# A ninth slot for raw weights, denser gate steps, and a new order in the wide places of an expert pipeline

## The chip, the cores and the metric

One core of a Trainium2 chip (trn2). The time is that of the whole program on the device in microseconds, once per run; the profiled execution is one run of its own. TensorE (PE) multiplies, VectorE (DVE) and ScalarE (ACT) work on tiles in SBUF and PSUM, GpSimd (POOL) here issues the indirect transfers, SyncE (SP) issues the plain ones, and sixteen DMA engines move the bytes.

## What is computed

One layer of a streaming encoder over 512 tokens of width 1024: a norm, one wide projection, two kinds of attention, an output projection with residual, and then a mixture of 32 experts, of which every token uses 4. All but the last part takes the first quarter of the time. The expert part, cut to what matters:

```python
logits = (hf @ w_router + b_router).astype(jnp.float32)
top_vals, top_idx = lax.top_k(logits, TOP_EXPERTS)       # 4 of 32
gates = jax.nn.softmax(top_vals, axis=-1)
...
def expert_block(args):
    tok, g, e = args
    xb = h_pad[tok]                                      # the tokens of expert e
    gu = xb @ w_gu[e] + b_gu[e]                          # 1024 -> 2048
    glu = jnp.minimum(gu[:, :D_EXPERT], SWIGLU_LIMIT)
    lin = jnp.clip(gu[:, D_EXPERT:], -SWIGLU_LIMIT, SWIGLU_LIMIT)
    act = glu * jax.nn.sigmoid(SWIGLU_ALPHA * glu) * (lin + 1.0)
    return (act @ w_down[e] + b_down[e]) * g[:, None].astype(h.dtype)
```

## The kernel before, in words

**Chunks.** The weights of an expert are 12 MB in float32, read in 12 chunks of 1 MB (128 partitions x 2048): eight of the gate and up weights (c = 0 to 7, `NG`) and four of the down weights (c = 8 to 11). `chunk_no` numbers all 384 in the order in which they are used: the gate and up chunks of expert i, then the down chunks of expert i - 1, then those of i + 1, and so on. Number 0 to 7 are the first expert's, 8 to 15 the second's.

**The path of a chunk.** SP loads it into one of `RAW` = 8 raw slots (`load_chunk`, line 825); the slot is chunk number modulo `RAW`, and SP waits until VectorE is done with the chunk that had the slot before. ScalarE rounds it to a high half (`split_hi`, line 833) into one of `HL` = 4 buffers `whl`; it waits for the landing, and for TensorE's use of the chunk four before. VectorE subtracts, which gives the low half (`split_lo`, line 838), and frees the raw slot. TensorE multiplies both halves (`chunk_products`, line 2125). Precision of float32 is had this way from products of rounded halves. All transfers of weights are in SP's one queue.

**Wide and narrow.** The 32 experts are put in an order (`place_experts`) in which 17 places are wide (up to 128 rows; three products per pair of halves, 12 matmuls of 512 columns to a chunk) and 15 are narrow (`NARROW`: 3, 4, 7, 8, 11, 12 ... 27, 28, 30; up to 64 rows, whose high and low rows share the array, 8 matmuls to a chunk, and two folds add the halves up). The first three experts are fixed; the others depend on the counts.

**Order within place i.** Each engine has its own queue, written out by hand. PE: bias and eight gate and up chunks of expert i (`gate_up`), among them the transposes of the activations of i - 1 (`turn_a`) and the search for the rows of i + 2 (`find_both`); transposes of the gathered rows of i + 1 (`turn_x`); bias and four down chunks of i - 1 (`down`). ACT (`act_round`): the eight high halves, then those of the down chunks 8 to 10; the gate (`gated`, line 1314), the high halves of the transposed rows (`turn_x_hi`, 1296), the selector (`pick_gu`), and then the high half of the twelfth chunk, c = 11. DVE (`dve_round`): eight low halves, three more, the clamp of the linear part (`lin`, line 1798), the low halves of the transposed rows (`turn_x_lo`, 1779), the product of gate and linear part (`activate`, 1806), and then the twelfth low half. In narrow places the twelfth halves stand ahead of `gated` and `lin` already. GpSimd gathers the rows of i + 2 (line 1019) and adds the results of i - 2 to the output (line 1028), both indirect, in its own queue.

**The start of the expert part.** After the last token block is routed, VectorE makes the ranks, finds the rows of experts 0 and 1, then spreads the gates over the experts (`spread_gates`): softmax over the 4 chosen, a comparison of 512 columns, a product of 512, a sum to 128, and then copies that `turn_g` transposes. Only after that does it come to the first low half. Chunks 0 to 5 are loaded ahead, 6 and 7 after the last normalised rows have been written to DRAM; chunk 8 waits for the first low half. GpSimd clears the first gather buffer `xg0` as soon as attention is over, and prepares small tables (`tie`, `ordered`, `spread`, `left`) behind that. PE runs filler matmuls (`keep_warm`) between the short steps.

**Memory.** Addresses are laid out by hand. `xg0` lies at `o_qb + 54272`, the scratch of the gates (`one`, `onek`) and the scratch of the row search `ohd` just above it, the transposed gate table `gT` at `o_qb + 12288`, where the raw biases `bg_raw` were.

## Time and profile before

| what | us |
|---|---|
| median of 3 runs (1439.07 to 1441.06) | 1440.77 |
| the profiled execution | 1441.15 |
| its span | 1439.0 |
| PE busy in the span | 1348.1 (94%) |
| DVE busy | 1254.8 (87%) |
| ACT busy | 1118.7 (78%) |
| POOL busy | 207.4 (14%) |
| VectorE's low halves of the weights, 384 of 2286 ns | 862.9 |
| ScalarE's high halves, 384 of 1916 ns | 725.8 |
| read from DRAM | 440.89 MB |

The page cuts the span into 40 slices of 36 us and gives the busy share of each engine as a digit; 9 is 90% or more. The expert part begins in the tenth slice, near 340 us. In the answers quoted below `idle before <-X` is the time that an engine stood idle ahead of an instruction and what ended it. Busy times of PE are modelled from pipelined matmuls. A wait is put down to the last of several releasers.

### The profile page before, as it was taken

How to read it: one execution, taken by the hardware profiler on the slowest of the kernel's cores; microseconds unless marked ns; L12 is line 12 of the kernel's file. 1: busy time of each engine (PE TensorE's matmuls, PEld its weight loads, DVE VectorE, ACT ScalarE, POOL GpSimd, SP SyncE). 2: the span in 40 equal slices, each digit the busy share in tenths (PEclk: the TensorE clock that was granted, in tenths of full speed). 3: DMA queues.
4: the chain of work that ended last, by engine and by line, in shares of the span. 5: the costliest groups of instructions: out<-in, count | busy, mean ns of one | idle time of the engine just before them, and what ended most of it. 6: DMA issues, size and time to landing. Idle time of an engine off the chain costs nothing. (4 is left out here: it accounts for less than half of the span.)

```text
span 1439.0 us, 18474 instructions
## 1 busy us (share of the span) xinstructions
PE 1348.1 (94%) x6573; PEld 1089.5 (76%) x6576; DVE 1254.8 (87%) x1314; ACT 1118.7 (78%) x1225; POOL 207.4 (14%) x134
## 2 busy tenths in 40 slices
PE   6999878999999999999998999999899989998996
PEld 5887766776787878778876887787778768876785
DVE  4799779548989999999899998999999999899995
ACT  5666564455788988988898888888888988898884
POOL 1112000011011211111210111111111111210131
PEclk9999979999999999999999999999999999999999
DMA  5422111148899999999999999999999999999992
GB/s 153 146 74 59 33 71 45 44 159 310 337 348 363 409 411 387 394 403 391 390 395 396 392 375 401 394 389 379 403 383 390 382 389 388 393 387 386 398 396 66
DMA packets 85349, 446.41 MB, mean 310 GB/s; under 512 B 18432, under 2 KB 23552, under 8 KB 36032
## 3 DMA queue, kind: packets, MB, share of 16 engines
q1 hardware_dynamic: 73424, 428.32, 75.1%
q0 software_dynamic: 9216, 16.81, 4.6%
q8 instruction: 54, 0.88, 0.2%
q10 hardware_dynamic: 2608, 0.01, 0.1%
q14 instruction: 47, 0.39, 0.1%
HBM read 440.89 MB, written 20.97 MB: 321 GB/s over the span
## 5 line engine op out<-in xcount | busy, mean ns | idle before, releaser
L838 DVE TENSOR_TENSOR whl<-wraw,whl 128x2048 fp32r<-128x2048 f32 x384 | 862.9, 2286 | 73.1 <-ACT whl L833 71.7
L833 ACT ACTIVATE whl<-wraw 128x2048 fp32r<-128x2048 f32 x384 | 725.8, 1916 | 136.8 <-PE ps L2125 88.2
L2125 PE MATMUL ps<-whl,xT 128*128 128x512 f32 x2640 | 634.0, 394 | 13.6 <-DVE whl L838 11.6
L2125 PEld LDWEIGHTS ps<-whl,xT 128*128 128x128 f32 x2640 | 488.5, 188 | 129.3 <-DVE whl L838 19.4
L2125 PE MATMUL ps<-whl,aT 128*128 128x512 f32 x1248 | 297.9, 394 | 5.2 <-DVE whl L838 5.2
L2125 PEld LDWEIGHTS ps<-whl,aT 128*128 128x128 f32 x1248 | 235.5, 190 | 60.4 <-DVE whl L838 10.1
L1028 POOL DMA_INDIRECT out_dram<-ysb,idx x32 | 84.5, 2641 | 667.2 <-ACT ysb L1325 667.2
L1019 POOL DMA_INDIRECT xg<-h_rows,idx x32 | 80.0, 2501 | 262.5 <-DVE idx L1767 258.5
L1879 PE MATMUL ps<-W,HT 128*128 128x512 f32 (+1 forms) x184 | 73.9, 402 | 5.4 <-DVE W L610 4.4
L1881 PE MATMUL ps<-W,HT 128*128 128x512 f32 (+1 forms) x184 | 70.3, 382 | 0.0
L1880 PE MATMUL ps<-W,HT 128*128 128x512 f32 (+1 forms) x184 | 70.3, 382 | 0.0
L1507 DVE TENSOR_REDUCE nmax<-ps 128x1 f32<-128x128 f32 (+3 forms) x64 | 31.2, 487 | 30.8 <-PE ps L1953 30.0
L1314 ACT ACTIVATE acts<-ps 128x1024 f32<-128x1024 f32 x32 | 32.9, 1030 | 16.7 <-PE ps L2125 15.2
L1879 PEld LDWEIGHTS ps<-W,HT 128*128 128x128 f32 x184 | 36.5, 198 | 11.1 <-issue 5.2
L2082 PE MATMUL ps<-ident,xg 128*128 128x128 f32 x256 | 34.0, 276 | 9.0 <-DVE gslot L1773 7.7
L2082 PEld LDWEIGHTS ps<-ident,xg 128*128 128x128 f32 x256 | 28.6, 140 | 17.9 <-DVE gslot L1773 13.7
L1169 ACT ACTIVATE raw<-ps,nmax 128x384 f32<-128x384 f32 (+2 forms) x40 | 24.1, 604 | 22.5 <-DVE nmax L1507 22.3
L1325 ACT ACTIVATE ysb<-ps,gslot 128x1024 f32<-128x1024 f32 x32 | 35.1, 1098 | 8.3 <-DMA out_dram<-ysb,idx 7.3
L1881 PEld LDWEIGHTS ps<-W,HT 128*128 128x128 f32 x184 | 36.4, 198 | 6.7
L1179 ACT ACTIVATE sq<-ps 128x384 f32<-128x384 f32 (+2 forms) x28 | 14.7, 524 | 34.5 <-PE ps L1891 34.2
L1806 DVE SCALAR_TENSOR_TENSOR acts<-acts 128x1024 f32<-128x1024 f32 x32 | 39.1, 1221 | 1.5
L1880 PEld LDWEIGHTS ps<-W,HT 128*128 128x128 f32 x184 | 36.7, 199 | 4.6
(294 smaller groups left out, 1428.3 us busy)
## 6 DMA issues: line engine op xcount, KB each, us to landing
wraw<-in_w_gu_dram SPq DMA_DIRECT2D x256, 1024.0 KB, 15.5
wraw<-in_w_down_dram SPq DMA_DIRECT2D x128, 1024.0 KB, 13.5
WR<-in_w_in_dram SPq DMA_DIRECT2D x20, 512.0 KB, 3.8
WR<-in_w_o_dram SPq DMA_DIRECT2D x8, 512.0 KB, 4.0
xs<-in_x_dram SPq DMA_DIRECT2D x4, 512.0 KB, 8.1
WR<-in_x_dram SPq DMA_DIRECT2D x4, 512.0 KB, 3.6
out_dram<-WR SPq DMA_DIRECT2D x4, 512.0 KB, 2.6
h_rows<-WR SPq DMA_DIRECT2D x4, 512.0 KB, 2.6
```

Source lines behind the costliest of these rows:

```text
L833: act.activation(whl[:, n % HL, 0, :], wraw[n % RAW], ACT.Copy).then_inc(chunk_hi, 1)
L838: eng.tensor_tensor(whl[:, n % HL, 1, :], wraw[n % RAW], whl[:, n % HL, 0, :].bitcast(F32), ALU.subtract).then_inc(chunk_lo, 1)
L1019: pool.indirect_dma_start(xg[j % 2], None, hd, bass.IndirectOffsetOnAxis(ap=idx[:, j:j + 1], axis=0), bounds_check=SEQ - 1, oob_is_err=Fal ...
L1028: pool.indirect_dma_start(out[0], bass.IndirectOffsetOnAxis(ap=idx[:, e:e + 1], axis=0), ysb, None, bounds_check=SEQ - 1, oob_is_err=False ...
L1314: act.activation(acts[:, 0, :].rearrange("p (a n) -> p a n", a=2), ps[:, GU:GU + 2, :], ACT.Gelu_apprx_sigmoid).then_inc(sig_ok, 1)
L1325: act.activation(ysb.rearrange("p (a n) -> p a n", a=2), ps[:, dn_bank(e):dn_bank(e) + 2, :], ACT.Copy, scale=gslot[:, e:e + 1]).then_inc( ...
L1806: dve.scalar_tensor_tensor(out=acts[:, 2, :], in0=acts[:, 0, :], scalar=GLU_TOP, in1=acts[:, 1, :], op0=ALU.min, op1=ALU.mult).then_inc(ac ...
L1879: pe.matmul(dst, a[0], b[0], start=k_first, stop=False)
L1880: pe.matmul(dst, a[0], b[1], start=False, stop=False)
L1881: return pe.matmul(dst, a[1], b[0], start=False, stop=k_last)
L2082: ins = pe.transpose(ps[:, TP + b, k * P:(k + 1) * P], xg[j % 2][:, (4 * b + k) * P:(4 * b + k + 1) * P], ident)
L2125: ins = pe.matmul(bank, a[x_][j], w[:, b, j, 512 * q:512 * q + 512], start=False, stop=last and j == nj - 1 and n == len(parts) - 1)
```

## The change

- `RAW` goes from 8 to 9. The ninth slot takes the place of `xg0` and the gates' scratch; SP waits for the chunk nine before, and the stream's first load without a wait is chunk 8. The count of landings to wait for is worked out per slot.
- `xg0` moves onto the raw biases, so GpSimd waits for the three steps of the biases (`bg_ok`, 3) before it clears it. `gT` moves into the last third of `acts`, `ohd` to a place of its own; `one`, `onek` and `gate` go.
- The gates: the difference to the largest logit, the exponential, a product with the 0/1 mask of chosen experts, sum, reciprocal and product are done over all 128 columns (4 blocks x 32 experts) instead of over the 16 chosen and then spread.
- In wide places the high half of the twelfth chunk comes before `gated` on ScalarE, and its low half right behind `lin`, ahead of the transposed rows and `activate`, on VectorE.

```diff
-RAW, HL = 8, 4
+RAW, HL = 9, 4
...
-        wraw = [place(f"wraw{s}", [P, 2048], F32, offset=base + 8192 * s if s < 6 else o_qb + 66560 + 8192 * (s - 6))
-                for s in range(RAW)]
+        wraw_at = [base + 8192 * s for s in range(6)] + [o_qb + 66560, o_qb + 74752, o_qb + 54272]
+        wraw = [place(f"wraw{s}", [P, 2048], F32, offset=wraw_at[s]) for s in range(RAW)]
...
-        xg0 = place("xg0", [P, D], F32, offset=o_qb + 54272)
+        xg0 = place("xg0", [P, D], F32, offset=o_qb + 12288)
...
-        gT = place("gT", [3 * E, 2, T * P], F32R, offset=o_qb + 12288)
+        gT = place("gT", [3 * E, 2, T * P], F32R, offset=o_qb + 40960)
...
         def load_chunk(eng, r, e, c, at_=None):
             n = chunk_no(e, c)
             w = wraw[n % RAW]
-            after(eng, chunk_lo, PER_ROUND * r + n - RAW + 1)
+            after(eng, chunk_lo, PER_ROUND * r + max(n - RAW + 1, 0))
...
-            act.wait_ge(landed[n % RAW], 16 * (PER_ROUND // RAW * r + n // RAW + 1))
+            per_slot = len(range(n % RAW, PER_ROUND, RAW))
+            act.wait_ge(landed[n % RAW], 16 * (per_slot * r + n // RAW + 1))
...
-                    if not is0(r) or chunk_no(e, c) >= RAW:
+                    if not is0(r) or chunk_no(e, c) >= NG:
                         load_chunk(sp, r, e, c, ids_at.get(e))
...
             pool.wait_ge(values_ok, values_no("A", T - 1, HA - 1))
+            pool.wait_ge(bg_ok, 3)
             pool.memset(xg[0], 0.0).then_inc(xg_clear, 1)
...
-            act.activation(gate, gate, ACT.Exp).then_inc(gates_exp, 1)
+            act.activation(gden, gden, ACT.Exp).then_inc(gates_exp, 1)
...
                     if narrow(i):
                         gu_low_half(r, i)
                     else:
+                        split_hi(act, r, i - 1, NCH - 1)
                         gated(r, i)
                     if i + 1 < E:
                         turn_x_hi(r, i + 1)
                         pick_gu(r, i + 1)
-                    split_hi(act, r, i - 1, NCH - 1)
                     if narrow(i):
+                        split_hi(act, r, i - 1, NCH - 1)
                         gated(r, i)
...
-            dve.tensor_tensor(gate, top8[:, :, 0:TOPE], top8[:, :, 0:1].to_broadcast([P, T, TOPE]),
-                              ALU.subtract).then_inc(gates_in, 1)
+            dve.tensor_tensor(gden, lg, top8[:, :, 0:1].to_broadcast([P, T, E]), ALU.subtract).then_inc(gates_in, 1)
...
                 dve.wait_ge(gates_exp, 1)
-                link(dve.tensor_reduce(gsum, gate, AX.X, ALU.add))
+                link(dve.tensor_tensor(gden, gden, selm, ALU.mult))
+                link(dve.tensor_reduce(gsum, gden, AX.X, ALU.add))
                 link(dve.reciprocal(gsum, gsum))
-                link(dve.tensor_tensor(gate, gate, gsum.unsqueeze(2).to_broadcast([P, T, TOPE]), ALU.mult))
-                link(dve.tensor_tensor(one.rearrange("p t k e -> p (t k) e"),
-                                       over_experts(0, E), over_choices(idxf, E), ALU.is_equal))
-                link(dve.tensor_tensor(onek.rearrange("p t k e -> p (t k) e"),
-                                       one.rearrange("p t k e -> p (t k) e"), over_choices(gate, E), ALU.mult))
-                link(dve.tensor_reduce(gden, onek.rearrange("p t k e -> p t e k"), AX.X, ALU.add))
+                link(dve.tensor_tensor(gden, gden, gsum.unsqueeze(2).to_broadcast([P, T, E]), ALU.mult))
...
                     if not narrow(i):
                         lin(r, i)
+                        split_lo(dve, r, i - 1, NCH - 1)
                     if i + 1 < E:
                         turn_x_lo(r, i + 1)
                     if narrow(i):
                         split_lo(dve, r, i - 1, NCH - 1)
                         lin(r, i)
                     activate(r, i)
-                    if not narrow(i):
-                        split_lo(dve, r, i - 1, NCH - 1)
```

## Rows read from the trace of the kernel before

**Rows 1.** The page, slices of 36 us: busy tenths of the DMA engines

```profile
DMA  5422111148899999999999999999999999999992
```

**Rows 2.** Stretches: length, PE, PEld, DVE, ACT, POOL busy, clock, DMA share, GB/s

```profile
500.00:600.00 100.00, 97.50 (x456) 78.69 (x455) 93.92 (x61) 86.67 (x76) 14.44 (x6) 1.00 1.00 396
700.00:800.00 100.00, 94.26 (x437) 74.84 (x436) 92.31 (x60) 86.65 (x75) 13.09 (x6) 1.00 0.99 393
```

**Rows 3.** Groups, 500 to 1400 us: instruction, count | busy, mean ns | idle before

```profile
L838 DVE TENSOR_TENSOR whl<-wraw,whl 128x2048 fp32r<-128x2048 f32 x322 | 723.1, 2286 | 63.3 <-ACT whl L833 62.2
L833 ACT ACTIVATE whl<-wraw 128x2048 fp32r<-128x2048 f32 x322 | 608.6, 1917 | 114.6 <-PE ps L2125 67.6 <-DMA wraw<-in_w_down_dram 42.5 <-DMA wraw<-in_w_gu_dram 4.0
```

**Rows 4.** Weight loads, issue to landing, issued 345-412, 412-460, 600-1400 us

```profile
DMA to landing us min/median/max: 4.8/5.2/6.6
...
DMA to landing us min/median/max: 6.5/7.8/9.1
...
DMA to landing us min/median/max: 12.2/15.6/18.6
```

**Rows 5.** Stretches of 4 us behind expert 10, columns as in rows 2

```profile
704.00:708.00 4.00, 4.00 (x20) 3.30 (x19) 4.00 (x3) 3.05 (x2) 0.00 (x0) 1.00 0.85 349
732.00:736.00 4.00, 4.00 (x19) 3.27 (x18) 2.76 (x3) 4.00 (x5) 0.69 (x1) 1.00 1.00 424
```

**Rows 6.** Timeline, start of the experts: start, length, engine, line [idle before]

```profile
340.71 0.69 DVE L1684 TENSOR_TENSOR onek<-one,gate 128x512 f32<-128x512 f32 x1
341.43 1.04 DVE L1686 TENSOR_REDUCE gden<-onek 128x128 f32<-128x512 f32 x1
344.23 1.07 PE L2082 MATMUL ps<-ident,xg 128*128 128x128 f32 x8 [0.80 <-DMA xg<-h_rows,idx]
346.01 1.27 PE L2153 MATMUL ps<-bgs,sel 128*128 128x512 f32 x4
```

**Rows 7.** Gathers into xg, issue to landing: the first; those of 500-1400 us

```profile
DMA to landing us min/median/max: 4.0/4.0/4.0
...
DMA to landing us min/median/max: 9.9/10.2/10.6
```

**Rows 8.** Timeline, transposes of the rows of expert 1

```profile
371.67 1.06 PE L2082 MATMUL ps<-ident,xg 128*128 128x128 f32 x8 [0.45 <-issue]
```

**Rows 9.** Timeline, VectorE at expert 1: the clamp, and the twelfth half

```profile
401.38 1.22 DVE L1798 TENSOR_SCALAR acts<-ps 128x1024 f32<-128x1024 f32 x1
404.84 6.69 DVE L838 TENSOR_TENSOR whl<-wraw,whl 128x2048 fp32r<-128x2048 f32 x3
```

**Rows 10.** Three weight loads: ns of issuing, first and last start; issue to landing

```profile
L825 SPq DMA_DIRECT2D wraw<-in_w_gu_dram x1: 328/328/328, 407.2 to 407.2; - x1
...
L825 SPq DMA_DIRECT2D wraw<-in_w_down_dram x1: 327/327/327, 409.4 to 409.4; - x1
...
DMA to landing us min/median/max: 5.1/5.1/5.1
...
L825 SPq DMA_DIRECT2D wraw<-in_w_down_dram x1: 328/328/328, 411.6 to 411.6; - x1
...
DMA to landing us min/median/max: 5.9/5.9/5.9
```

**Rows 11.** Timeline at expert 13: splits after the product, PE's twelfth chunk, next bias

```profile
806.05 11.09 DVE L838 TENSOR_TENSOR whl<-wraw,whl 128x2048 fp32r<-128x2048 f32 x5
808.39 2.11 PE L2125 MATMUL ps<-whl,aT 128*128 128x512 f32 x8 [0.55 <-DVE whl L838]
810.33 1.07 PE L2153 MATMUL ps<-bgs,sel 128*128 128x512 f32 x4
```

**Rows 12.** Timeline at the last expert, and the last rows

```profile
1409.38 1.23 DVE L1806 SCALAR_TENSOR_TENSOR acts<-acts 128x1024 f32<-128x1024 f32 x1
...
1412.73 1.28 DVE L1790 TENSOR_TENSOR xT<-ps,xT 128x512 fp32r<-128x512 f32 x2
...
1428.27 1.11 ACT L1325 ACTIVATE ysb<-ps,gslot 128x1024 f32<-128x1024 f32 x1 [7.29 <-DMA out_dram<-ysb,idx]
```

More of the change, by code:

```diff
@@ L391, in build @@
         at["free"] = kept
-        one = place("one", [P, T, TOPE, E], F32, offset=o_qb + 58368)
-        onek = place("onek", [P, T, TOPE, E], F32, offset=o_qb + 60416)
         gden = place("gden", [P, T, E], F32, offset=o_qb + 62464)
@@ L400, in build @@
         gfcol = place("gfcol", [P, KD], F32)
+        ohd = place("ohd", [P, T, P], BF16, offset=at["free"])
         gh = place("gh", [P, 5, HD], F32)
@@ L439, in build @@
         idxf = place("idxf", [P, T, TOPE], F32)
-        gate = place("gate", [P, T, TOPE], F32)
         gsum = place("gsum", [P, T], F32)
@@ L452, in build @@
         passed = place("passed", [P, 2 * E], U32)
-        ohd = place("ohd", [P, T, P], BF16, offset=o_qb + 58368)
         cmax = place("cmax", [P, 1], F32)
@@ L1668, in read_counts @@
                 dve.tensor_copy(crow, ps[:, TP + 1, T * E:(T + 1) * E]).then_inc(counts_read, 1)
-            def over_experts(e0, n):
-                return iota[:, e0:e0 + n].unsqueeze(1).to_broadcast([P, T * TOPE, n])
-            def over_choices(tile, n):
-                return tile.rearrange("p t k -> p (t k)").unsqueeze(2).to_broadcast([P, T * TOPE, n])
             def spread_gates():
                 dve.wait_ge(gates_exp, 1)
-                link(dve.tensor_reduce(gsum, gate, AX.X, ALU.add))
+                link(dve.tensor_tensor(gden, gden, selm, ALU.mult))
+                link(dve.tensor_reduce(gsum, gden, AX.X, ALU.add))
                 link(dve.reciprocal(gsum, gsum))
-                link(dve.tensor_tensor(gate, gate, gsum.unsqueeze(2).to_broadcast([P, T, TOPE]), ALU.mult))
-                link(dve.tensor_tensor(one.rearrange("p t k e -> p (t k) e"),
-                                       over_experts(0, E), over_choices(idxf, E), ALU.is_equal))
-                link(dve.tensor_tensor(onek.rearrange("p t k e -> p (t k) e"),
-                                       one.rearrange("p t k e -> p (t k) e"), over_choices(gate, E), ALU.mult))
-                link(dve.tensor_reduce(gden, onek.rearrange("p t k e -> p t e k"), AX.X, ALU.add))
+                link(dve.tensor_tensor(gden, gden, gsum.unsqueeze(2).to_broadcast([P, T, E]), ALU.mult))
                 dve.tensor_copy(gdup[:, :, 0:2, :], gden.unsqueeze(2).to_broadcast([P, T, 2, E])).then_inc(gdup_ok, 1)
```

## The prediction

> **What bounds the kernel now.** I read the page's slices first [rows 1]: from the ninth slice on, which is the expert stage, the DMA digit stays at 9 until the last slice. The stretches of 100 us [rows 2] say it more sharply: the DMA engines are busy 0.99 to 1.00 of the time, TensorE 94 to 98 us of 100, VectorE 92 to 94 (one early and one later stretch stand there). Nothing has room, so which is the bound must be read from who is late. The groups of instructions [rows 3] show that ScalarE, whose high halves start each chunk's work, waits 42.5 + 4.0 us for landings and 67.6 us for TensorE (its four split buffers); VectorE waits only for ScalarE. So in some places a weight chunk is late and in others TensorE is.
>
> The decisive view is the time from the issue of a weight load to its landing [rows 4]. Each load is 1 MB and is issued when VectorE has finished with the chunk eight before it. Where the DMA engines had run dry, a load lands in 4.8 us (345 to 412 us). From 600 us on it takes 12.2 us at least and 15.6 in the median. A megabyte takes 2.47 us at the best rate that the stretches of 4 us show (1.049 MB / 424 GB/s, [rows 5]), so even the quickest load finds about (12.2 - 4.8) / 2.47 = 3 others ahead of it, and the median 4 to 5. After about 412 us the engine that delivers the last part of each load therefore never stands idle. That it is one lagging part and not all 16 follows from the other row of [rows 5]: at 704 to 708 us the mean busy share is 0.85 while loads still wait 12 us. Some engines had emptied every issued load; the last one had not. A load counts as landed only with its last part, so the rate of the slowest engine sets the rate of the stage.
>
> The Trainium skill (DMA: Bandwidth & Descriptors, Latency and other measured facts) says that two of the sixteen DMA engines are usually slower in traces, with the reason uncertain. The views here have no time for a single engine, so the trace bears out the inequality but not which engine.
>
> **Part 1, the ninth slot.** It lets each load be issued one VectorE split earlier. While the last engine is always busy that changes the order of nothing: a longer queue in front of the same server. It pays only once, in the stage's first 70 us, where loads land in 4.8 to 6.6 us and TensorE is the bound. The last time that the engines run dry in the kernel before is around 407 to 412 us. The load issued at 411.6 us lands after 5.9 us, at 417.5 [rows 10]. With nine slots it may be issued when the load before it was, at 409.4, the end of the first split of expert 2. If it finds the engines dry it lands 5.1 us later [rows 10], at 414.5: 3.0 us earlier. If the load ahead of it is still under way (issued at 407.2 at the earliest without a new order, [rows 10]; 5.1 us later it is 412.3, then 2.47 to 3.1 for the next), it lands at 415.0: 2.5 earlier. From there on no load waits for a slot, and every later landing, the last one too, keeps that lead. The order of part 3 decides between the two: at expert 1, a wide place, VectorE makes the twelfth lower half at 404.84 now, behind the clamp (401.38, 1.22 us), the transposed rows and the product [rows 9]. Moved ahead of rows and product it ends at about 404.8 instead of 407.1, so the load ahead is issued 2.3 us earlier. I take **-2.9 us**, with -2.5 as the bound without that help.
>
> **Part 2, the start.** The gates lose four DVE steps over 128 x 512 and over 16 columns and gain three over 128 x 128. Of the removed ones the comparison and the product, of one shape, took 0.69 us each and the sum 1.04 [rows 6]; the new ones are near the 0.2 to 0.3 us of steps of that size. VectorE reaches its first split about 2.1 us sooner. The cover of this saving is TensorE: its first transposes wait for the gathered rows until 344.23 (0.80 us idle, <-DMA), and then it is in steady work through the bias products (346.01, 1.27 us) up to the first expert product at 347.3 [rows 6]. So the saving ends in a wait for the rows, and is worth nothing at 347. The VectorE queue then runs about half a microsecond ahead, which removes the 0.45 us wait of TensorE at 371.67 [rows 8] (for the permuted tables, that VectorE reads behind two splits): worth 0.2 to 0.4 us.
>
> Against it stands chunk 8. Before, it waited for VectorE's first split; now it goes out right behind chunks 6 and 7, ahead of the first gather. In the kernel before the gather landed in 4.0 us; among full queues later it takes 9.9 to 10.6 [rows 7]. No run shows it with one load beside it. The load holds each engine for 2.47 us and nothing more is issued before VectorE's first split ends at about 344, so the gather can be 0 to 2.5 us late. I take 1.5, nearer the upper end, since [rows 7] shows that gathers do wait behind weight loads. Every step after it up to 412 us is a TensorE chain, so this delays the consumer, and with it the slots and all later landings: 1.5 less the 0.2 above, **+1.3 us**, bounds -0.4 and +2.3.
>
> The Trainium skill (DMA: Bandwidth & Descriptors, Queues, rings and completion order) says that a DMA engine takes turns between its queues packet by packet, a packet being a bundle of rows. By that rule the gather would wait for one whole packet of the load at most, which is the 2.5 us end; by single rows it would be nearer 1 us.
>
> The moved memory costs nothing that I find: the clearing of the first gather buffer now waits for the bias splits, and these end on VectorE some five microseconds before GpSimd gets there; the gate table in the last third of the activations is read before the first product of activations is written.
>
> **Part 3, the order in wide places.** It moves no work away, only one high half (1.92 us of ScalarE) and one low half (2.29 us of VectorE, [rows 3]) ahead of gate, rows and product, 17 times. What is queued behind: the gate, the transposed rows and the selector on ScalarE, rows and product on VectorE. Who waits for those is TensorE, with the next expert's bias (needs the product) and first chunk (needs the rows). Where the expert before is narrow TensorE gets there soonest: at expert 13 the bias of the next runs at 810.33, while the product is ready at about 806.1 now (the five splits that follow it start at 806.05) and at 808.4 then, by the 2.29 us of a split [rows 3, 11]. There the move takes away a wait of 0.55 us for the twelfth lower half at 808.39 [rows 11], 7 such places, 4 us of TensorE's time. With the DMA as the bound this is given back as waiting for landings in the narrow places: 0. If the DMA had room it would count in full. Landings allow the move: in the wide places ScalarE stands behind TensorE and not behind the twelfth chunk's landing (its long landing waits all stand in narrow ones).
>
> At the last place it costs. Expert 31 has no transposed rows to put in the gap. Now: product 1409.38 to 1410.6, twelfth lower half to 1412.8 (2.29 us, [rows 3]), which covers transposes and high half of the activations, their lower halves from 1412.73 (1.28 us), and then the next split [rows 12]. After: half from 1409.3 to 1411.5, product to 1412.75, and then the transposes (start to high half 0.8 us, high half 0.6) stand uncovered; the lower halves start at about 1414.2 instead of 1412.73. The chain goes on through the first down chunk of 31, the fold, the rows of 30, and their scatter, for which the last rows wait 7.29 us [rows 12]; all of it moves by **+1.5 us** (bounds 0 and +2.2, the whole move of the product).
>
> **Sum.** -2.9 + 1.3 + 1.5 = -0.1 us on the profiled execution of 1441.15 us (span 1439.0, 2.15 around it). The median of the three runs is 0.38 lower, so 1440.77 - 0.1 = 1440.7 us. The unknown terms at their ends give -2.9 - 0.4 + 0 = -3.3 and -2.5 + 2.3 + 2.2 = +2.0, so 1437.5 to 1442.8.
>
> **Rivals.**
> A, the mean of the engines binds and not the last one: then slot and order fill the dips, such as the 15% of 704 to 708 us [rows 5]. The stretches of 100 us leave 0 to 2% idle, 1% in the mean [rows 2], over 900 us some 9 us, and the start and end terms still cost 2.8 less the 2.9: 1440.7 - 9 = 1431.7. For it: the dips do fall behind wide places, where VectorE frees no slot for five microseconds. Against: the 12.2 us minimum [rows 4]. Chance 0.14.
> B, the terms at start and end come out at their lower bounds (the gather isn't disturbed, the gap at the end is covered): 1437.5, faster by 0.23%. Chance 0.09.
> C, slower: the first gather is caught as the later ones are. It then takes 10.2 us and not 4.0 [rows 7], TensorE's first expert product comes 6.2 us late, and 6.0 - 2.9 + 1.5 = +4.6: 1445.4. It decides at a gather over 4.5 us late. Against it: only one extra load is there to wait for. Chance 0.08.
> D, the ninth slot isn't used as said (a load still waits for an older split, or the lead is lost before 412 us): -2.9 drops out, 1443.6, at the edge of slower. Chance 0.05.
>
> **How the numbers follow.** The forecast, 1440.7 within 1437.5 and 1442.8, has 0.64; A 0.14, B 0.09, C 0.08, D 0.05. A measurement of this kernel tells about 0.2% (2.9 us) from no change. Faster: A, B, half of what the forecast has below 1438: 0.26. Slower: C, half of D and a little above the forecast's end: 0.12. Same: 0.62. The range leaves out A's better part and C: 1433.0 to 1443.5.
>
> **What would show it.** Right: landings of 4.8 us gone after 405 us and the time from issue to landing up by about 2.5 us in the rest of the stage (median near 18), DMA share and GB/s unchanged; ScalarE's waits for landings about as long as now; the 0.55 us waits before the twelfth chunk gone; the first gather over 4.0 us; a gap on VectorE behind the last product. Wrong: ScalarE's 46 us of landing waits shrink by a third or more while GB/s rises (A); or the first expert product at 353 (C).

## The result, and the profile after

| | before | changed |
|---|---|---|
| median of 18 runs each, us | 1439.22 (1436.94 to 1441.21) | 1441.59 (1437.54 to 1446.27) |
| ratio of the changed kernel to the one before | | 1.0018 [1.0010, 1.0025] |
| the profiled execution | 1441.15 | 1437.54 |
| its span | 1439.0 | 1435.3 |

The change makes the kernel slower by 2.4 us (1.4 to 3.6 by the interval). The forecast was no difference, 1440.7 us, within 1433.0 and 1443.5. The two profiled executions say the opposite of the medians: that of the changed kernel was the quickest of its 18, 4 us below its median, and that of before lies 1.9 us above its own. Spans of the two traces must not be subtracted. What can be compared is stages, and for that more traces of both were taken (below). Two later executions, one of e9 with 2216.8 us and one of the kernel before with 1863.6 us, ran at a mean granted clock of 0.56 and 0.67 and are left out of the ratios.

The page of the changed kernel: span, busy times, the DMA engines' busy tenths, and weight loads with the median time from issue to landing.

```profile
span 1435.3 us, 18473 instructions
PE 1346.7 (94%) x6573; PEld 1088.1 (76%) x6576; DVE 1254.2 (87%) x1312; ACT 1118.1 (78%) x1225; POOL 211.0 (15%) x134
...
DMA  5422111148899999999999999999999999999991
...
wraw<-in_w_gu_dram SPq DMA_DIRECT2D x256, 1024.0 KB, 18.6
wraw<-in_w_down_dram SPq DMA_DIRECT2D x128, 1024.0 KB, 16.4
```

The same stretches of 100 us as in [rows 2], with the same columns:

```profile
500.00:600.00 100.00, 97.94 (x458) 79.05 (x457) 94.39 (x61) 86.65 (x76) 14.46 (x6) 1.00 1.00 396
700.00:800.00 100.00, 95.47 (x436) 75.99 (x436) 91.85 (x59) 86.20 (x75) 14.00 (x6) 0.98 1.00 393
```

The transfers move the same 396 and 393 GB/s as in [rows 2]. Weight loads from issue to landing, issued at 345 to 412, 412 to 460 and 600 to 1400 us, as in [rows 4]:

```profile
DMA to landing us min/median/max: 4.6/6.1/7.2
...
DMA to landing us min/median/max: 4.9/7.1/7.6
...
DMA to landing us min/median/max: 13.7/18.6/21.0
```

In the steady part a load is under way for 3.0 us more in the median, 18.6 against 15.6. That is about one load's time: 2.47 us at the best rate [rows 5], and 2.65 us at the 396 GB/s of the stage (1.049 MB / 396 GB/s, an estimate). The ninth slot is used, and what it holds is a place in a queue. The groups of 500 to 1400 us, as in [rows 3]: ScalarE's high halves, and TensorE's products.

```profile
L831 ACT ACTIVATE whl<-wraw 128x2048 fp32r<-128x2048 f32 x324 | 613.4, 1916 | 121.7 <-PE ps L2113 75.0 <-DMA wraw<-in_w_down_dram 41.6 <-DMA wraw<-in_w_gu_dram 5.0
...
L2113 PE MATMUL ps<-whl,aT 128*128 128x512 f32 x1059 | 251.0, 393 | 1.5 <-DVE whl L836 1.4
```

ScalarE waits 41.6 + 5.0 us for landings, where it was 42.5 + 4.0. TensorE's wait for low halves is 1.4 us in that stretch; in the kernel before the same group stood idle for 5.2 us, so nearly all of the 4 us of waits for the twelfth lower half [rows 11] are gone. ScalarE's waits for TensorE grew from 67.6 to 75.0 us in the same stretch; what the order is worth in time is taken up below.

The start. The first gather from issue to landing (4.0 us in [rows 7]), and TensorE's first transposes with the idle time ahead of them (0.80 us in [rows 6]):

```profile
DMA to landing us min/median/max: 6.4/6.4/6.4
...
343.44 1.06 PE L2070 MATMUL ps<-ident,xg 128*128 128x128 f32 x8 [2.87 <-DMA xg<-h_rows,idx]
```

The end, the timeline at the last expert, which answers to [rows 12]: start, length, engine, line, idle time ahead.

```profile
1399.78 3.79 PE L2113 MATMUL ps<-whl,aT 128*128 128x512 f32 x16
...
1402.44 2.28 DVE L836 TENSOR_TENSOR whl<-wraw,whl 128x2048 fp32r<-128x2048 f32 x1
1404.64 1.22 DVE L1795 SCALAR_TENSOR_TENSOR acts<-acts 128x1024 f32<-128x1024 f32 x1
1405.91 1.16 PE L2079 MATMUL ps<-ident,acts 128*128 128x128 f32 x8 [2.34 <-DVE acts L1795]
1406.82 5.51 PE L2113 MATMUL ps<-whl,aT 128*128 128x512 f32 x16
1407.35 1.29 DVE L1779 TENSOR_TENSOR xT<-ps,xT 128x512 fp32r<-128x512 f32 x2 [1.50 <-ACT xT L1305]
...
1424.22 1.11 ACT L1324 ACTIVATE ysb<-ps,gslot 128x1024 f32<-128x1024 f32 x1 [7.07 <-PE ps L2113]
```

The low half now runs ahead of the product (L1795), the product is 2.28 us later, and nothing covers that: TensorE stands idle for 2.34 us ahead of the transposes of the activations, and VectorE for 1.50 us behind the product. Then comes something that the forecast did not have. Sixteen matmuls took 3.79 us at 1399.78, and 5.51 us at 1406.82. The stretches of the same part (columns as in [rows 2]) show why:

```profile
1399.00:1406.00 7.00, 4.66 (x22) 3.54 (x21) 6.76 (x4) 4.69 (x4) 0.00 (x0) 1.00 0.18 75
1406.00:1411.00 5.00, 5.00 (x19) 4.14 (x20) 3.65 (x4) 3.43 (x4) 0.00 (x0) 0.66 0.03 15
1411.00:1416.00 5.00, 5.00 (x23) 4.11 (x22) 5.00 (x3) 4.20 (x3) 0.00 (x0) 1.00 0.00 0
```

The granted clock is 1.00 up to the wait and 0.66 in the 5 us behind it, so most of that stretch was at 1.2 GHz instead of 2.4. TensorE had stood idle for 2.34 us before. The transposes right behind the wait still took 1.16 us, as in the kernels with the old last place; the low clock came after them. The Trainium skill (TensorE: Matmul & The Clock Gate, HAM oscillation — how this bites in real kernels) describes a kernel whose TensorE waits some 3 to 5 us for data in every round and comes back at the lower clock. This trace is like it in kind, with 0.66 behind a shorter wait; in e10 (below) the clock is 1.00 behind a wait of 2.36 us, so it is seen here in some traces and not in all.

### The profile page after: what moved, and what is told of

It is laid out like the page before. It is cut to its first block and busy times, and to the rows that moved or that the text cites. A ratio compares the mean times of both kernels' runs of the same rounds, so it can differ in the third digit from the quotient of the medians.

```text
span 1435.3 us, 18473 instructions
## 1 busy us (share of the span) xinstructions
PE 1346.7 (94%) x6573; PEld 1088.1 (76%) x6576; DVE 1254.2 (87%) x1312; ACT 1118.1 (78%) x1225; POOL 211.0 (15%) x134
## 5 line engine op out<-in xcount | busy, mean ns | idle before, releaser
L1018 POOL DMA_INDIRECT xg<-h_rows,idx x32 | 84.6, 2643 | 262.1 <-DVE idx L1756 258.1
L1795 DVE SCALAR_TENSOR_TENSOR acts<-acts 128x1024 f32<-128x1024 f32 x32 | 39.0, 1220 | 1.5
L970 POOL TENSOR_TENSOR rstd<-ss,half 128x8 f32<-128x8 f32 (+1 forms) x16 | 23.3, 1458 | 107.1 <-DVE ss L1429 107.1
## 6 DMA issues: line engine op xcount, KB each, us to landing
wraw<-in_w_gu_dram SPq DMA_DIRECT2D x256, 1024.0 KB, 18.6
```

The costliest lines, as they stand in the source:

```text
L1018: pool.indirect_dma_start(xg[j % 2], None, hd, bass.IndirectOffsetOnAxis(ap=idx[:, j:j + 1], axis=0), bounds_check=SEQ - 1, oob_is_err=Fal ...
L1795: dve.scalar_tensor_tensor(out=acts[:, 2, :], in0=acts[:, 0, :], scalar=GLU_TOP, in1=acts[:, 1, :], op0=ALU.min, op1=ALU.mult).then_inc(ac ...
```

## Stages of all traces

Two marks cut the expert stage: the first high half of the stage (chunk 0) and that of chunk 376, the first down chunk of expert 30, eight chunks from the last. In the changed kernel they are

```profile
328.93 3.70 ACT L831 ACTIVATE whl<-wraw 128x2048 fp32r<-128x2048 f32 x2
...
1392.23 1.92 ACT L831 ACTIVATE whl<-wraw 128x2048 fp32r<-128x2048 f32 x1 [1.61 <-DMA wraw<-in_w_down_dram]
```

so 1063.30 us lie between them, and 43.1 us from the second to the end of the span. A third mark, chunk 16, is the first down chunk; it stands behind the gate and up chunks of the first two experts. The same for every trace, in us; the experiments are told below.

| trace | slots | last place | chunk 0 to 16 | chunk 0 to 376 | chunk 376 to end | chunk 0 to end |
|---|---|---|---|---|---|---|
| before | 8 | old | 59.75 | 1067.19 | 40.0 | 1107.2 |
| before, second trace | 8 | old | 58.40 | 1064.69 | 40.6 | 1105.3 |
| changed | 9 | new | 60.03 | 1063.30 | 43.1 | 1106.4 |
| changed, second trace | 9 | new | 60.00 | 1063.06 | 43.0 | 1106.1 |
| e2, last place as before | 9 | old | 59.94 | 1063.17 | 40.9 | 1104.1 |
| e3, all places as before | 9 | old | 59.80 | 1063.89 | 40.9 | 1104.8 |
| e4, before with the new order | 8 | new | 58.45 | 1063.86 | 43.0 | 1106.9 |
| e6, as e2 | 8 | old | 58.12 | 1063.97 | 40.9 | 1104.9 |
| e7, as e2 | 7 | old | 57.90 | 1066.39 | 40.5 | 1106.9 |
| e9, as e2, gather first | 9 | old | 59.41 | 1063.32 | 40.8 | 1104.1 |
| e10, before, new last place | 8 | new | 58.45 | 1066.73 | 42.2 | 1108.9 |
| e11, changed, filler at the end | 9 | new | 63.20 | 1066.76 | 42.1 | 1108.9 |

Chunk 0 itself comes at 328.9 to 333.7 us, whatever the kernel; the part ahead of it makes most of the difference between executions. Three of the traces are disturbed between the first marks: in that of before, from which the forecast was made, and in that of e9 TensorE's granted clock was 0.79 in the mean of 374 to 382 us (some 1.4 us lost, by 59.75 against 58.40), and e11 had a low clock twice (below). The other rows agree to 0.3 us in the first column for either number of slots, and to 0.9 in the last but one for either last place. In between executions differ by up to 2 us: e10, whose change lies behind chunk 376, needs 1066.73 us up to there, and the second trace of before 1064.69. The clock goes with that. From 632 to 640 us the granted clock is 0.79 in e10 and in the first trace of before, which need 1008.3 and 1007.4 us from chunk 16 to 376; it is 1.00 in the other three traces with eight slots (the second of before, e4, e6), which need 1005.4 to 1006.3. No run shows that this is the whole of the difference.

The same marks show when the loads become the bound. ScalarE's first wait for a landing comes at 593 us in e6 and at 623 us in the changed kernel. Up to chunk 80, at 568 us, the changed kernel stays 1.9 us behind e6, counted from chunk 0; at chunk 150, at 758 us, it is 0.9 us ahead. So the delay of the start is seen at once and in full, and the lead of the slot only where landings are waited for.

## Experiments

Ratios are to the kernel before, run on the same chip beside them; medians are of 11 or 12 runs unless said. The kernel before had medians of 1439.58 (e1 to e4), 1439.96 (e5 to e8) and 1440.08 (e9 to e12). An interval is about 0.001 to either side, so the difference of two ratios is good to some 0.0014, 2 us.

**e1, the changed kernel again**, without an edit.

> The changed kernel once more, for its distance to the kernel before and for a second profile of it. Its first profiled execution (1437.5 us) was its quickest of 18, four below their median, so what makes the usual execution slower has not been seen yet. Theory 1 (loss at the end of the program): ratio 1.001 to 1.0025 again, and in the trace the lead of 3 to 4 us of the expert stage is there until the last expert and is lost there. Theory 2 (the ninth load in the queues slows the transfers in some executions): the second trace shows the stage between 600 and 1400 us longer than in the kernel before by 2 to 5 us. Either way the landing time of the loads has a median of 18 to 19 us.

Measured: 1441.80 us, 1.0020 [1.0007, 1.0033]. The loss is of the kernel. The second theory is out: the stage up to chunk 376 is as short as in the first trace (1063.06 us). The first holds for the end (43.0 us), but the lead up to there is 1.6 us against e5 (below) and not 3 to 4.

**e2, the last place as before.** The changed kernel, with the old order at i = E - 1 alone.

```diff
                     else:
-                        split_hi(act, r, i - 1, NCH - 1)
+                        if i < E - 1:
+                            split_hi(act, r, i - 1, NCH - 1)
                         gated(r, i)
+                        if i == E - 1:
+                            split_hi(act, r, i - 1, NCH - 1)
...
                         lin(r, i)
-                        split_lo(dve, r, i - 1, NCH - 1)
+                        if i < E - 1:
+                            split_lo(dve, r, i - 1, NCH - 1)
...
                     activate(r, i)
+                    if i == E - 1:
+                        split_lo(dve, r, i - 1, NCH - 1)
```

> The changed kernel with the old order in the last place alone (expert 31: gate and product ahead of the twelfth halves), the new order in the other 16 wide places. Theory 1: the trace of the changed kernel lost 3.1 us there (1.5 for the uncovered transposes, 1.6 for matmuls at half clock behind TensorE's wait of 2.3 us), so this comes out 3.1 us below the changed kernel, about 0.7 below the kernel before (ratio 0.9995). Theory 2: only 1.5 to 3 below the changed kernel's, and the scatter from run to run stays.

Measured: 1438.87 us, 0.9999 [0.9990, 1.0008]; 2.9 us below e1. Its timeline at the end, the transposes of the last activations and the products behind them:

```profile
1405.65 1.16 PE L2085 MATMUL ps<-ident,acts 128*128 128x128 f32 x8 [0.18 <-DVE acts L1798]
1406.57 3.92 PE L2119 MATMUL ps<-whl,aT 128*128 128x512 f32 x16
```

The wait of 2.34 us is 0.18 and the matmuls take 3.92 us, not 5.51. By the table the end is 40.9 instead of 43.0 us. With one place of the seventeen undone the whole net loss is gone.

**e3, the old order in all wide places**, nine slots and the new gates kept: the two moves of the change undone for every i.

> The changed kernel with the old order in all wide places: nine slots, moved memory and the new gate steps alone. Theory 1: the lead of the slot without the end's loss, 2.5 less 0.3 at the start: 2.2 us below the kernel before (ratio 0.9985). Theory 2: the slot is what costs, so it is 1 to 3 us above the kernel before (ratio 1.001 to 1.002) and scatters by 8 us as the changed kernel does.

Measured: 1440.04 us, 1.0002 [0.9991, 1.0013]. The gain that I expected of slots and gates alone isn't there. Against e2 it is 1.2 us slower by the medians and 0.7 by the traces (1104.8 against 1104.1): small, and inside the intervals.

**e4, the new order alone.** The kernel before with the moves of the change in all wide places, eight slots, old gates.

> The kernel before, with eight slots and its old gate steps, and only the new order in the wide places. Theory 1: no lead (at most 0.2 us from the earlier slot at expert 1) and the whole loss at the end: 3 us above the kernel before (ratio 1.002). Theory 2: only the 1.5 us of the end, ratio 1.001, with the small scatter of the kernel before.

Measured: 1440.48 us, 1.0011 [1.0000, 1.0023]. The end takes 43.0 us as in the changed kernel. Up to chunk 376 it needs 1063.86 us, 0.8 less than the undisturbed trace of before. Its ratio is that of e10 below, which moves the last place alone (1.0011 and 1.0012), so by the medians the other sixteen places are worth nothing.

**e5, the kernel before, a second trace.** One run.

> The kernel before, once more, for a second trace of it: four kernels with parts of the change, one with eight slots among them, were all about 3.3 to 4 us ahead of its first trace at the last expert, which a slot can't explain. Theory: the first trace of the kernel before was an unlucky one (half clock for 3.4 us at 374 us and again at 634 us), and this one gets to the high half of chunk 376 some 1065.5 us after that of chunk 0 (the first took 1067.2), so that the real lead of the changed kernel is 2 to 2.5 us. Rival: 1067 again, the lead is 4 us and is lost elsewhere.

Measured: 1437.50 us; 1064.69 us from chunk 0 to 376, where I had expected 1065.5. Against this trace the changed kernel reaches chunk 376 1.4 to 1.6 us sooner, and not 3.9.

**e6, eight slots, and e7, seven**, in the kernel of e2.

```diff
-RAW, HL = 9, 4
+RAW, HL = 8, 4
```

> The changed kernel with the old order at the last expert (the one that took 1438.9) and eight slots instead of nine, all else equal (moved memory, new gate steps, new order in 16 wide places). Theory 1 (a longer queue before the same last DMA engine, lead won once): 2.5 us more, 1441.4. Rival (the slot's lead is lost or was never bound): no more than 0.5 us.

> The same with seven slots. Theory 1: another 2.5 us, 1444, and the quickest landing after 600 us takes about 10 us. Rival (the slots hold a reserve that the wide and narrow places use up in turn): several times that, 1450 and more.

Measured: eight 1439.03 us, 0.9991 [0.9982, 1.0000]; seven 1440.74, 1.0008 [0.9997, 1.0018]; nine (e2) 1438.87, 0.9999 [0.9990, 1.0008]. Weight loads issued at 600 to 1400 us, from issue to landing, with seven slots and with eight (nine: 18.6 in the median, above):

```profile
DMA to landing us min/median/max: 9.8/13.2/15.9
...
DMA to landing us min/median/max: 12.3/15.9/18.5
```

Each slot adds 2.7 us of waiting, one load's time, and no throughput. What is left of a slot is the lead that it wins once. From seven to eight it is 1066.39 - 1063.97 = 2.4 us in the traces and 1.7 us by the medians. From eight to nine it is 0.8 net; the first two experts take 1.8 us more with nine (59.94 against 58.12), so without that the lead is 2.6 us. Both expectations were too high: e6 by 2.4 us, since with the ninth slot the late gather goes too, and e7 by 3.3 us, most of it the same error carried on.

**e8, lighter loads.** The kernel of e2; the loads of down chunks bring only 512 of each 1024 columns, a sixth of all weight bytes less, and the other half of such a slot is what lay there.

```diff
-            eng.dma_start(w if c < NG else w.rearrange("p (j n) -> p j n", j=2),
-                          chunk_src(e, c, at_)) \
+            eng.dma_start(w if c < NG else w.rearrange("p (j n) -> p j n", j=2)[:, :, 0:512],
+                          chunk_src(e, c, at_) if c < NG else chunk_src(e, c, at_)[:, :, 0:512]) \
```

> The same kernel with nine slots, where every load of a down chunk brings only half of its columns (the other half of the slot keeps what an earlier chunk left); all other work is the same. Its output is not the reference's for that. That is 67 MB less, 158 us of the DMA engines' time at 424 GB/s. Theory 1: the bound becomes TensorE and VectorE, and the 42 to 46 us of ScalarE's waits for landings go, so 30 to 45 us less. If TensorE were the bound: under 5 us less. Landings take about 5 to 7 us throughout.

Measured: 1415.01 us (2 runs), 0.9824 [0.9806, 0.9842], 24 us below e2. The stretch of 700 to 800 us, columns as before:

```profile
700.00:800.00 100.00, 97.83 (x458) 79.01 (x457) 96.15 (x64) 91.06 (x81) 19.13 (x6) 1.00 0.95 349
```

The loads carry the stage: fewer bytes, less time. Between 450 and 1400 us no wait of ScalarE for a landing is left. But the gain is less than the 30 to 45 us expected, with TensorE (97.83) and VectorE (96.15) right behind, and from 600 us on a load still takes 7.9 us in the median to land, where 5 to 7 were expected.

**e12, lighter TensorE.** The kernel of e2 without the third product of the down chunks in wide places, so a part of the precision of these products is left out: 272 matmuls, some 63 us of TensorE's work by 0.23 us each; its busy time on the page falls by 41 us, from 1347.2 to 1305.9.

```diff
-                parts = ((0, 0), (0, 1)) if narrow(e) else ((0, 0), (0, 1), (1, 0))
+                parts = ((0, 0), (0, 1)) if narrow(e) or c >= NG else ((0, 0), (0, 1), (1, 0))
```

> Nine slots and old order at the last expert, and the third product (low half of the activations by high half of the weights) of all down chunks in wide places is left out: 17 x 16 matmuls of 0.23 us, 63 us of TensorE's time. Its output is not the reference's for that. Theory 1 (DMA is the bound after the first experts): only the chain up to 412 us gets shorter, and little after it: 5 to 12 us less in all. Rival (TensorE binds in wide places and DMA in narrow ones, without reserve between them): 30 us less or more. Halving the down loads gave 25 us, less than the 30 to 45 expected, so TensorE and VectorE stand close behind the DMA.

Measured: 1435.74 us (8 runs), 0.9971 [0.9959, 0.9982], 3.1 us below e2. The same stretch:

```profile
700.00:800.00 100.00, 88.71 (x404) 68.02 (x403) 91.56 (x60) 85.34 (x73) 12.65 (x6) 1.00 1.00 392
```

TensorE falls to 88.71 us, and DMA stays at 1.00 and 392 GB/s. The 41 to 63 us of TensorE bring 3 (4 by the ratios), less than the 5 to 12 expected; a sixth of the bytes brings 24. The rival by which TensorE is the bound (some 30 us) is out.

**e9, the gather first.** The kernel of e2; chunk 8 is issued only when the first gather has landed.

```diff
+                    if is0(r) and chunk_no(e, c) == NG:
+                        sp.wait_ge(gathered[0], 16)
                     if not is0(r) or chunk_no(e, c) >= NG:
                         load_chunk(sp, r, e, c, ids_at.get(e))
```

> Nine slots, old order at the last expert, new order in the other wide places, and one more wait: SyncE issues chunk 8 only when the first gather has landed. Theory 1 (the ninth load holds up the first gather: 6.3 us instead of 4.0 to 4.5, TensorE 1.8 us late): the first expert product comes 1.8 us sooner after the first high half, and the lead of the slot stays, since the DMA engines run dry many times before 412 us anyway; 1.8 us below the kernel without this wait (1438.9), so 1437.1, and 2.3 us below the kernel before (ratio 0.9983). Rival (the late start has another cause, the new gate steps or the moved memory): no change, or slower by what chunk 8 loses.

Measured: 1436.53 us (1436.48 without the execution of 2216.8 us), 0.9972 [0.9962, 0.9982], where 1437.1 was expected. The first gather and TensorE's first transposes:

```profile
DMA to landing us min/median/max: 4.4/4.4/4.4
...
345.39 1.06 PE L2078 MATMUL ps<-ident,xg 128*128 128x128 f32 x8 [0.88 <-DMA xg<-h_rows,idx]
```

In e2 the gather takes 6.3 us and the transposes wait 2.78; here it is 4.4 and 0.88, as with eight slots (4.5 and 0.92 in e6). Among all kernels of this study this is the quickest but for those that leave work out, 3.6 us below the kernel before and 5 below the changed one. It has the ninth slot and the new order, and neither of the two costs. Its trace doesn't show the gain: with 1439.3 us it is the slowest of the 11 executions compared, it lost some 1.4 us at 374 us, and from chunk 0 to the end it takes 1104.1 us like e2. The gain stands on the medians.

**e10, the new last place alone**, in the kernel before: both twelfth halves moved as in the change, at i = E - 1 only.

> The kernel before with the new order in the last place alone (expert 31). Theory 1: all of the loss at the end and none of the rest, 2.3 to 2.9 us above the kernel before (ratio 1.0016 to 1.002), a TensorE wait of 2.2 us ahead of the last transposes in the trace, half clock behind it, and now and then an execution at 1444 or more. Rival (the loss needs the fuller queues of nine slots too): under 1 us.

Measured: 1441.62 us, 1.0012 [1.0002, 1.0022], +1.5 us. Its end takes 42.2 us. The same two rows as for e2:

```profile
1413.74 1.16 PE L2096 MATMUL ps<-ident,acts 128*128 128x128 f32 x8 [2.36 <-DVE acts L1809]
1414.66 3.93 PE L2130 MATMUL ps<-whl,aT 128*128 128x512 f32 x16
```

TensorE waits as long as in the changed kernel, 2.36 us, but this time the products run at full clock in 3.93 us. The end is 42.2 - 40.6 = 1.6 us longer than in the second trace of before. That is the uncovered latency by itself; against the ends of all traces with the old last place (40.0 to 40.9) it is 1.3 to 2.2 us. By the median 1.5 us came where 2.3 to 2.9 were expected, which the interval of the ratio (0.3 to 3.2 us) leaves open; the expected low clock isn't in this trace. Of the four traces with this wait and no filler, three have the low clock behind it (the two of the changed kernel and e4); none of the traces with the old last place has it there.

**e11, a warm TensorE at the end.** The changed kernel with ten filler matmuls into an unused part of PSUM ahead of the last `turn_a`.

```diff
                     if e == E - 2 and c == NG + 1:
+                        for _ in range(10):
+                            pe.matmul(ps[:, TP, :], identb, ones.unsqueeze(1).to_broadcast([P, T, P]),
+                                      start=True, stop=True)
                         turn_a(r, E - 1)
```

> The changed kernel with 10 filler matmuls on TensorE, into a PSUM bank that the transposes then overwrite, in the wait ahead of the last transposes of activations. It parts the loss at the end in two. Theory 1 (1.5 us of uncovered transposes and 0.8 to 1.6 us of half clock behind TensorE's idle 2.3 us): the second part goes, 1 to 1.6 us below the changed kernel (1441.7), and with it the executions at 1444 to 1446. Rival (the clock falls there by its own count of time, or costs nothing on the path): as the changed kernel.

Measured: 1441.75 us, 1.0016 [1.0003, 1.0029]. The filler, the transposes and the products:

```profile
1408.21 2.33 PE L2182 MATMUL ps<-ones,identb 128*128 128x512 bf16 x10
1410.73 1.16 PE L2079 MATMUL ps<-ident,acts 128*128 128x128 f32 x8 [0.18 <-DVE acts L1795]
1411.64 3.91 PE L2113 MATMUL ps<-whl,aT 128*128 128x512 f32 x16
```

The low clock is gone (3.91 us) and the end is down from 43.0 to 42.1 us, as it should be. The median didn't follow: 1 to 1.6 us less were expected, and 0.05 came by the medians, 0.6 by the ratios. With 2 us of doubt in either that decides nothing. The executions of 1444 us and more, which were expected to go, did not: two of twelve. Its trace shows a trouble at the start: transposes, filler, bias and the stretches around them.

```profile
345.11 1.47 PE L2070 MATMUL ps<-ident,xg 128*128 128x128 f32 x8 [3.20 <-DMA xg<-h_rows,idx]
346.63 1.87 PE L1874 MATMUL ps<-ones,identb 128*128 128x512 bf16 x4
347.94 1.79 PE L2141 MATMUL ps<-bgs,sel 128*128 128x512 f32 x4
...
346.00:350.00 4.00, 4.00 (x21) 2.73 (x20) 3.45 (x3) 0.97 (x2) 0.00 (x0) 0.62 0.47 199
374.00:382.00 8.00, 6.13 (x24) 4.88 (x23) 7.76 (x11) 7.09 (x11) 0.00 (x0) 0.79 0.55 215
```

TensorE waited 3.20 us for the gathered rows; then the clock was 0.62 from 346 to 350 us, and 0.79 once more from 374 to 382. In the changed kernel's first trace both stretches have 1.00. The two low stretches cost this execution 3.2 us (63.20 against 60.0 up to chunk 16).

## Why the prediction was wrong

The sum was -2.9 + 1.3 + 1.5 = -0.1 us, and the kernel became 2.4 us slower. The steps that failed are the sizes of the two losses, the late gather and the last place. Both were too small in the sum, and together they outweigh the lead of the slot. What the runs say for each term, by the traces (stages) and by the ratios of neighbouring kernels (good to 2 us each):

| term | forecast | by traces | by ratios x 1440 |
|---|---|---|---|
| lead of the ninth slot | -2.9 | -2.6 (e6 to e2, without the start) | -2.7 (0.9991 of e6 to 0.9972 of e9) |
| late gather | +1.3 | +1.8 (e6 to e2, chunk 16) | +3.9 (0.9972 of e9 to 0.9999 of e2) |
| last place | +1.5 | +2.2 (e2 to changed), +1.6 without the low clock (e10) | +3.0 (0.9999 of e2 to 1.0020 of e1) |
| order in the other places, gates | 0 | -0.4 (e6 against before's second trace) | -1.3 (before to 0.9991 of e6) |
| sum | -0.1 | +1.0 | +2.9 |

The right-hand column must sum to the loss measured in e1, since each kernel is compared with the next; the middle one need not, and it falls short.

**Right.** The bound, and the way it was read. Loads that never land in under 12.2 us [rows 4] where an idle path needs 4.8 mean a queue that never runs empty there; e7, e6 and e2 show 13.2, 15.9 and 18.6 us for seven, eight and nine slots at no more throughput, and e12 that 41 to 63 us of TensorE are worth 3. The lead was to be won once and to be 2.5 to 2.9 us: 2.6. The landing times from 600 us on, the unchanged GB/s, ScalarE's waits (46.6 us, was 46.5), the vanished 0.55 us waits, the later gather and the gap behind the last product all came as listed. One sign did not: landings of 4.8 us were to be gone after 405 us, and between 412 and 460 us the quickest takes 4.9 us in the changed kernel's first trace and 5.0 in the second of before. So "after about 412 us never idle" was a reading of one trace; the engines still run dry some tens of us later, which moves the place of the lead and not its size. Rival A (the mean of the engines binds) is out, since GB/s didn't rise; so is C, with a gather 2.4 us late and not 6.2; so is D, since the queue is one load longer; and B, since neither term came out at its lower bound.

**The late gather was mis-sized.** The step "0 to 2.5 us late, I take 1.5" was the first that failed. It is 1.9 to 2.4 us late (6.3 and 6.4 us against 4.0 to 4.5), close to the whole load of 2.47 us, and the first two experts are 1.8 us longer instead of 1.3. The prediction held the upper end, 2.5 us, against 1.5, and the upper end was the better number. It had it from the turn-taking packet by packet of the Trainium skill (DMA: Bandwidth & Descriptors, Queues, rings and completion order), with the whole of a load's share on an engine taken as one packet. The 1.9 to 2.4 us agree with that reading. No view here shows how much of a load goes between two turns, and behind full queues the gather took 10.2 us [rows 7], far more than one load, so the rule alone doesn't give the number.

**The last place was mis-sized.** The latency was right: 1.5 predicted, 1.6 without the clock (e10; 1.3 to 2.2 by the trace it is compared with). The step that failed is that I followed the chain with today's durations. I wrote that the transposes would stand uncovered and did not ask what TensorE does meanwhile: it stands idle for 2.3 us in the middle of the last expert, and in the two traces of the changed kernel and in e4 the products behind it ran partly at 1.2 GHz (5.51, 5.45 and 4.80 us, where 3.8 is the rule). With that the end is 2.2 us longer.

**The other wide places and the gates, put at 0, are worth little.** Without the late gather and with the old last place, new order and new gates show 0.9991 [0.9982, 1.0000] (e6). By that 0.4 (traces) to 1.3 us (ratio) were gained in sixteen wide places and the gates; e3 against e2 puts 0.7 to 1.2 of it on the order, e4 against e10 none. Each of these is within the doubt of a ratio. That is small against the 4 us of waits that it removed, so "given back as waiting for landings" holds for most of them.

**The trace of before.** It had 1.4 us of low clock at 374 us and ran 1.9 us over its median. The terms were differences inside this trace. But the base of the forecast was the median of three runs, 1440.77 us; with the 18-run median of 1439.2 in its place the same sum gives 1439.1, 2.5 us off and not 0.9. That 1440.7 came so near to 1441.6 is luck: a base too high made up for losses taken too small.

**What stays open.** The stages of the traces account for some +1.0 us, the medians for +2.4 (interval 1.4 to 3.6). By the table the missing part would lie with the late gather (1.8 us in the traces, 3.9 by the ratios) and the last place (2.2 and 3.0), but each of these ratios is good to 2 us only. A cause is at hand for a part of it. 7 of the 29 executions of the changed kernel took 1444 us or more; none of the compared ones of the kernel before did (the highest is 1442.9). None of the seven was traced, but the mean granted clock of each execution is known: 0.978 or 0.979 in all seven, and 0.981 to 0.985 in the other 22. A mean lower by 0.004 is some 6 us of full-clock time in 1440 (an estimate), about what they are longer. So these seven had more of the low clock. Without them the medians of the changed kernel are 1441.1 and 1441.5 us, 1.9 above the kernel before each time, so they make up some 0.5 of the missing 1.4 us. Where in them the clock was low is not shown. Behind a wait of some 3 us for the gathered rows it can be, as in e11, where that cost 3.2 us; against that place stands that e2 and e3 have the late gather too, and none of their 22 executions reached 1444 us. The low clock isn't the only cause of slow executions either: e4 has one of 1446.0 us and e10 one of 1444.4 at a mean of 0.982. The traced one of e10 had the full clock at the start and at the end; it lost its time ahead of chunk 0 (at 333.3 us) and in the middle of the stage.

## What to carry to other kernels

- Before a prefetch is made deeper, read the time from issue to landing. Where it is several times that of an idle path everywhere, one more slot lengthens a queue by one load's time. It pays once, and the extra load may stand in front of something small that is urgent: here a gather. With the last place as before, one wait that holds the load back for it took the kernel from no difference to 3.6 us faster by the medians.
- A change of order that holds in a loop must be looked at apart for its last round. Here nothing follows that fills the gap: one place of seventeen cost 1.6 to 3.0 us, more than the other sixteen and the new gates won (0.4 to 1.3).
- For effects of 0.1 to 0.2% a single trace is no base for a difference. Two executions of the same kernel differed by 2.5 us between the same marks. Stages of two traces each, the granted clock in each stage, and medians do it together.

## What the runs showed of the hardware

- TensorE's granted clock after short waits is a matter of the execution. Behind waits of 2.3 to 2.4 us at the end it was 0.66 in the mean of 5 us in the changed kernel, and 1.00 in the same place of e10, with products of 3.93 us. Behind 2.87 us at the start it stayed at 1.00, behind 3.20 us it was 0.62 over 4 us. Ten filler matmuls in the wait at the end left 0.18 us of it, and the products took 3.91 us.
- Ahead of a gather a single 1 MB load costs 1.9 to 2.4 us; a full queue costs 6 (10.2 us in [rows 7]).
- The stage is nearer to a balance than 0.99 to 1.00 of DMA time says. With a sixth of the bytes gone the DMA share was still 0.95, at 349 GB/s instead of 393, and TensorE and VectorE had taken over.
